# A depthwise convolution split over three engines: one channel tile leaves TensorE, and 24 taps go as ScalarE products to accumulating DMAs

## The reference

```python
h = rms_norm(x, norm_g)
proj = jnp.einsum('bsd,de->bse', h, w_in)
a, bv, bg, z = jnp.split(proj, [A_W, A_W + B_W, A_W + 2 * B_W], axis=-1)
pooled = multiscale_pool(a.reshape(B, S, POOL_GROUPS, POOL_CH))      # trailing means of 2, 4, 8, 16
ya = jnp.einsum('bsgc,gce->bsge', pooled, pool_w).reshape(B, S, A_W) * pool_scale
u = bv * jax.nn.sigmoid(bg)
u = causal_depthwise_conv(u, conv_w, width=31) + conv_b              # one filter per channel
yb = jax.nn.silu(layer_norm(u, cn_g, cn_b))
y = jnp.concatenate([ya, yb], axis=-1) * jax.nn.silu(z)
x = x + jnp.einsum('bse,ed->bsd', y, w_out)
```

## Time and profile before

| | |
|---|---|
| median of 3 runs | 352.47 us (352.41 to 352.56) |
| profiled execution | 352.38 us, its span 350.6 us |
| PE busy | 342.6 us, 98% |
| DVE busy | 268.8 us, 77% |
| ACT busy | 212.7 us, 61% |
| POOL busy | 16.7 us, 5% |
| PE in the chain that ended last | 88% |
| DMA | 54.30 MB, mean 155 GB/s |
| granted clock of PE | full in all 40 slices |

### The profile page before, as it was taken

The page is one execution under the profiler, slowest core; times in us unless marked ns, Lnnn a source line. Parts: engine busy times, 40 slices in busy tenths (PEclk is TensorE's granted clock), DMA queues, the critical chain, the costliest instruction groups (busy, mean ns, idle before and its releaser), DMA issues.

```text
span 350.6 us, 5813 instructions
## 1 busy us (share of the span) xinstructions
PE 342.6 (98%) x2257; PEld 309.8 (88%) x2257; DVE 268.8 (77%) x512; ACT 212.7 (61%) x421; POOL 16.7 (5%) x26
## 2 busy tenths in 40 slices
PE   8999999999999999999999999999999999999995
PEld 8899999999999999998999999988887766688885
DVE  3998798999979999975877699774565686667533
ACT  5759999864239583044474664955359475675440
POOL 0000000000000000000000000004220030400000
PEclk9999999999999999999999999999999999999999
DMA  7896051560505156603625906383641523100003
GB/s 279 372 359 242 1 202 58 221 241 0 215 28 185 62 236 236 244 1 122 257 102 195 387 20 241 120 328 153 239 179 70 207 66 147 53 3 0 3 2 120
DMA packets 8235, 54.30 MB, mean 155 GB/s; under 512 B 912, under 2 KB 1040, under 8 KB 1936
## 3 DMA queue, kind: packets, MB, share of 16 engines
q1 hardware_dynamic: 8064, 53.78, 40.1%
q10 hardware_dynamic: 144, 0.15, 0.2%
HBM read 52.88 MB, written 1.05 MB: 154 GB/s over the span
## 4 chain that ended last, share of the span: by engine, by line
PE 88%; DVE 5%; DMA 2%; ACT 2%; issue 2%; SPq 0%; ACTq 0%; DVEq 0%
PE bank L963 20%; PE bank L965 20%; PE bank L964 20%; PE bank L995 16%; PE bank L1021 6%; DVE w_lo L633 3%; DMA raw<-w 2%; PE bank L1196 2%; PE bank L1206 2%; PE bank L1101 1%; PE bank L1220 1%; DVE scratch L882 1%; DVE scratch L873 1%; PE bank L1175 1%; PE bank L1038 1%
## 5 line engine op out<-in xcount | busy, mean ns | idle before, releaser
L633 DVE TENSOR_TENSOR w_lo<-raw,w_hi 128x1024 fp32r<-128x1024 f32 x76 | 89.2, 1219 | 12.1 <-ACT w_hi L369 12.0
L369 ACT CAST w_hi<-raw 128x1024 fp32r<-128x1024 f32 x76 | 75.3, 1048 | 6.4 <-PE bank L965 4.6
L744 DVE SCALAR_TENSOR_TENSOR scratch<-scratch,params 128x256 f32<-128x256 f32 x142 | 59.2, 476 | 3.5 <-ACT scratch L467 3.3
L963 PE MATMUL bank<-h_hi,w_hi 128*128 128x256 f32 x208 | 60.0, 288 | 0.0
L965 PE MATMUL bank<-h_hi,w_lo 128*128 128x256 f32 x208 | 58.8, 283 | 0.0
L964 PE MATMUL bank<-h_lo,w_hi 128*128 128x256 f32 x208 | 58.8, 283 | 0.0
L995 PE MATMUL bank<-H,raw 128*128 128x256 f32 x256 | 56.8, 379 | 0.9 <-DMA raw<-w 0.9
L995 PEld LDWEIGHTS bank<-H,raw 128*128 128x128 f32 x256 | 48.0, 190 | 7.3 <-DMA raw<-w 1.1
L963 PE MATMUL bank<-ya_hi,w_hi 128*128 128x256 f32 x144 | 42.8, 297 | 0.0
L965 PE MATMUL bank<-ya_hi,w_lo 128*128 128x256 f32 x144 | 40.7, 283 | 0.0
L964 PE MATMUL bank<-ya_lo,w_hi 128*128 128x256 f32 x144 | 40.7, 282 | 0.0
(11 more groups left out here) (116 smaller groups left out, 558.7 us busy)
## 6 DMA issues: line engine op xcount, KB each, us to landing
raw<-w SPq DMA_DIRECT2D x49, 1024.0 KB, 5.4
X<-xT SPq DMA_DIRECT2D x2, 512.0 KB, 5.1
out<-X SPq DMA_DIRECT2D x4, 256.0 KB, 2.7
consts<-const SPq DMA_DIRECT2D x1, 290.0 KB, 13.5
params<-vec ACTq DMA_DIRECT2D x1, 149.0 KB, 4.8
```

The source lines that it names most:

```text
L369: nc.scalar.copy(halves(w_hi, cut_slot(n), half), halves(raw, n % RAW, half)).then_inc(hi_cut, 1)
L633: nc.vector.tensor_tensor(halves(w_lo, cut_slot(n), half), halves(raw, n % RAW, half), halves(w_hi, cut_slot(n), half).bitcast(F32), ALU.s ...
L744: nc.vector.scalar_tensor_tensor(V[:, c, :], U[:, c, k:k + S], column(CW + TAPS * c + k), V[:, c, :], ALU.mult, ALU.add).then_inc(tap, 1)
L963: nc.tensor.matmul(dst, wh, ah, start=start, stop=False, skip_group_check=True)
```

## The change

Tile 7 leaves PE: the diagonals, the hi and lo parts of its taps and of its U, both calls of conv_taps, the read out of PSUM and all semaphores between them are gone. All eight tiles now are done in pairs.

Of pairs 0 and 1 (tiles 0 to 3), the last 12 taps (19 to 30) go another way. In each slot n from 2 on, ACT makes one "side item" for each such pair (12 slots each, from slot 2 and from slot 4): the product of one tap for both tiles, 128 x 512, in two instructions. The items take turns between two sums per pair in side_v. Items 0 and 1 are written to the sums themselves. Items 2 to 11 go to side_ring, and POOL issues a DMA that adds the slot of the ring to the sum (accum_op add), 20 DMAs of 256 KB from SBUF to SBUF. Before item 4 and later ones ACT waits for the DMA of the item two before, and so does POOL. DVE at last adds each of the four sums to V (128 x 512, "folds"), three slots after the last item of the sum or later.

conv_plan is new. It keeps an estimate of the time that DVE and ACT have left in each slot (slot_work) and takes the pair with the most taps left, a product where ACT has time and a single tap per tile where not. It begins at slot 2 instead of 3. It gives, slot by slot (single taps + products + folds): 2: 8, 3: 4+6, 4: 8, 5: 6+6, 6: 8, 7: 8+6, 8: 6, 9: 4+5, 10: 0+1, 11: 2+5, 12: none, 13: 6+3, 14: 4+2, 15: 6+5+1, 16: 8+0+1, 17: 8+0+1, 18: 6+0+1, 19: 10, 20: 12; in all 114 + 39 + 4. Before it was 142 single taps and 34 products, from slot 3 to slot 20.

channel_mean now goes through the tiles in the order 0 to 7. side_ring lies in the bytes of ya_lo, which is not in use in these slots.

```diff
+CONV_PAIRS = tuple((2 * i, 2 * i + 1) for i in range(4))
+SIDE = 2
+SIDE_ITEMS = 12
...
+def side_taps(pair):
+
+    return range(TAPS - SIDE_ITEMS, TAPS) if pair < SIDE else ()
+
+
+def side_items(n):
+
+    return [(pair, n - BG[pair + 1]) for pair in range(SIDE) if 0 <= n - BG[pair + 1] < SIDE_ITEMS]
+
+
+def slot_work(n):
+
+    dve, act = 0, 0.8 * len(side_items(n))
+    if n + 2 not in NATIVE and n < OA[0]:
+        dve, act = dve + 2.3, act + 1.9
+    if n - 1 in BV:
+        dve, act = dve + 0.6, act + 1.0
+    if n - 1 in A:
+        dve += 0.75 * (n - A[0]) + 1.0
+    if n in ZB or n - 1 in ZA:
+        dve, act = dve + 0.8, act + 0.6
+    if n in BG or n in A or n in ZB or n in ZA:
+        act += 0.6
+    if n in (ZB[0], PW):
+        act += 1.3 if n == ZB[0] else 3.2
+    return dve, act
 
 
 def conv_plan():
 
-
-
-
-
-    plan, last, used, count, rest = {}, {}, [], 0, conv_order()
-    for n in range(BV[1], OA[0] + 1):
+    plan, last, used, count, before = {}, {}, [], 0, None
+    left = {pair: [k for k in range(1, TAPS) if k not in side_taps(pair)] for pair in range(4)}
+    folds = list(range(2 * SIDE))
+    dve_time = act_time = 0.0
+    for n in range(BG[1], OA[0] + 1):
         plan[n] = []
-        budget = LONG_SLOT if n in (A[2] + 1, ZB[0] + 1) else SLOT
-        while rest and (budget > 0 or n == OA[0]):
-            g, k = rest[0]
-            tiles = CONV_GROUPS[g]
-            pair = tiles[0] // 2
-            if pair >= n // 2:
+        dve, act = slot_work(n)
+        length = 6.9 if n in NATIVE else 5.75
+        dve_time = min(dve_time, 2.0) + DVE_SHARE * length - dve
+        act_time = min(act_time, 2.0) + ACT_SHARE * length - act
+        while dve_time > 0 or n == OA[0]:
+            here = [pair for pair in left if left[pair] and CONV_PAIRS[pair][0] // 2 < n // 2]
+            if not here:
                 break
-            rest.pop(0)
-            if len(tiles) == 2 and k in PRODUCT_TAPS and pair < (n - 1) // 2 and A[0] - 3 <= n <= LAST_PRODUCT:
+            pair = max(here, key=lambda p: (len(left[p]) - (2 if p == before else 0), -p))
+            before, k, tiles = pair, left[pair].pop(0), CONV_PAIRS[pair]
+            if act_time > 0.8 and pair < (n - 1) // 2 and n <= LAST_PRODUCT:
                 count += 1
                 plan[n].append((tiles, k, len(used), max(last.get(c, 0) for c in tiles), count))
                 used.append(count)
-                budget -= 1.5
+                dve_time, act_time = dve_time - 0.61, act_time - 0.8
                 last.update({c: count for c in tiles})
             else:
                 for c in tiles:
                     count += 1
                     plan[n].append(((c,), k, None, last.get(c, 0), count))
                     last[c] = count
-                    budget -= 1
+                dve_time -= 0.8
+        while folds and n >= BG[folds[0] // 2 + 1] + SIDE_ITEMS + 1 + folds[0] % 2:
+            tiles = CONV_PAIRS[folds[0] // 2]
+            count += 1
+            plan[n].append((tiles, None, folds.pop(0), max(last[c] for c in tiles), count))
+            dve_time -= 0.61
+            last.update({c: count for c in tiles})
...
+        with nc.sbuf_tensor("side_ring", [P, SIDE, 2, 2, S], F32) as side_ring:
+            pass
         ya_lo = sb("ya_lo", [P, KD, S], F32R)
-        taps_hi = sb("taps_hi", [P, TAPS], F32R)
-        taps_lo = sb("taps_lo", [P, TAPS], F32R)
-        u_hi = sb("u_hi", [P, PAD + S], F32R)
-        u_lo = sb("u_lo", [P, PAD + S], F32R)
+        side_v = sb("side_v", [P, SIDE, 2, 2, S])
...
+            for n in range(BG[1], OA[0]):
+                for pair, item in side_items(n):
+                    if item > 1:
+                        pool.wait_ge(side_ready[pair], item + 1)
+                        if item > 3:
+                            pool.wait_ge(side_added[pair][item % 2], 16 * (item // 2 - 1))
+                        pool.dma_start(side_v[:, pair, item % 2, :, :], side_ring[:, pair, item % 2, :, :],
+                                       accum_op=ALU.add).then_inc(side_added[pair][item % 2], 16)
...
-            def build_diagonals(first, last):
-
-                for k in range(first, min(last, TAPS)):
-                    for part, t in zip(diagonals(k), (taps_hi, taps_lo)):
-                        nc.scalar.mul(part, ident, t[:, k:k + 1].bitcast(F32)).then_inc(diag_ready, 1)
+            def side_product(pair, item):
+
+                if item > 3:
+                    act.wait_ge(side_added[pair][item % 2], 16 * (item // 2 - 1))
+                to = (side_ring if item > 1 else side_v)[:, pair, item % 2, :, :]
+                k = side_taps(pair)[item]
+                for i, c in enumerate(CONV_PAIRS[pair]):
+                    last = nc.scalar.mul(to[:, i, :], U[:, c, k:k + S], column(CW + TAPS * c + k))
+                last.then_inc(side_ready[pair], 1)
...
+                for pair, item in side_items(n):
+                    side_product(pair, item)
...
+                    if k is None:
+                        pair, chain = divmod(product, 2)
+                        dve.wait_ge(side_added[pair][chain], 16 * ((SIDE_ITEMS - chain + 1) // 2 - 1))
+                        nc.vector.tensor_tensor(V[:, c:c + 2, :], V[:, c:c + 2, :], side_v[:, pair, chain, :, :],
+                                                ALU.add).then_inc(tap, 1)
+                    elif product is None:
...
-            def conv_taps(a, b):
-
-                pe.wait_ge(ulo_ready, 1)
-                pe.wait_ge(diag_ready, 2 * b)
-                for k in range(a, b):
-                    last = product(bank[5][:, 0:S], diagonals(k), (u_hi[:, k:k + S], u_lo[:, k:k + S]),
-                                   k == 0, k == TAPS - 1)
-                last.then_inc(conv_done, 1)
...
-                if n in (A[2], ZB[0]):
-                    conv_taps(*((0, CONV_CUT) if n == A[2] else (CONV_CUT, TAPS)))
...
-            def channel_mean(tiles):
-                for c in tiles:
-                    if c == CONV_PE:
-                        pe.wait_ge(conv_out, 1)
-                    else:
-                        pe.wait_ge(tap, TILE_DONE[c])
-                    last = nc.tensor.matmul(bank[1][:, 0:S], ones[:, :], V[:, c, :], start=(c == CONV_PE), stop=(c == 6),
+            def channel_mean():
+                for c in range(KD):
+                    pe.wait_ge(tap, TILE_DONE[c])
+                    last = nc.tensor.matmul(bank[1][:, 0:S], ones[:, :], V[:, c, :], start=(c == 0), stop=(c == KD - 1),
                                             skip_group_check=True)
-                if tiles[-1] == 6:
-                    last.then_inc(mean_sum, 1)
+                last.then_inc(mean_sum, 1)
```

More of the change, by code:

```diff
@@ L181, in conv_plan @@
                     last[c] = count
-                    budget -= 1
+                dve_time -= 0.8
[5 more added lines that the diff above has]
+            last.update({c: count for c in tiles})
     return plan, last, used
-SLOT, LONG_SLOT = 10, 14
-PRODUCT_TAPS = range(2, TAPS, 2)
+DVE_SHARE, ACT_SHARE = 0.97, 0.9
 CONV_PLAN, TILE_DONE, PRODUCT_USED = conv_plan()
@@ L226, in hybrid_trunk @@
         dist = C_[:, DIST:DIST + 384]
-        scratch = sb("scratch", [P, 12800])
+        scratch = sb("scratch", [P, 12654])
         at = 0
@@ L246, in hybrid_trunk @@
         FX = part(2 * 15).rearrange("p (c t) -> p c t", c=2)
-        assert at <= 12800
+        assert at <= 12654
         PR = SZ[:, 0:KD, :]
@@ L283, in hybrid_trunk @@
         late = sem("late")
-        taps_cut, uhi_ready, ulo_ready = sem("taps_cut"), sem("uhi_ready"), sem("ulo_ready")
-        diag_ready, conv_done, conv_out = sem("diag_ready"), sem("conv_done"), sem("conv_out")
+        side_ready = [sem(f"side_ready{i}") for i in range(SIDE)]
+        side_added = [[sem(f"side_added{i}{chain}") for chain in range(2)] for i in range(SIDE)]
         sig_ready, u_ready = sem("sig_ready"), sem("u_ready")
@@ L304, in hybrid_trunk @@
         block = ctx.enter_context(nc.Block())
[L306 to L310, removed]
         def column(c, n=1):
@@ L441, in _ @@
                     act.wait_ge(pooled, g + 1)
-                    if g == 0:
-                        act.wait_ge(conv_done, 2)
                     nc.scalar.copy(yb_hi[:, 2 * g:2 * g + 2, :], YP[:, 2 * g:2 * g + 2, :]).then_inc(phi_ready, 1)
                 for tiles, k, product, _, _ in CONV_PLAN.get(n, ()):
-                    if product is None:
+                    if product is None or k is None:
                         continue
@@ L463, in _ @@
                             act.wait_ge(u_ready, n // 2)
-                        if c == CONV_PE:
-                            nc.scalar.copy(u_hi[:, :], U[:, c, :]).then_inc(uhi_ready, 1)
-                        else:
-                            nc.scalar.activation(V[:, c, :], U[:, c, 0:S], ACT.Identity, bias=column(CB + c),
```

(14 more changed lines are left out.)

8 lines of the change are left out of this document (removed).

## The result

The changed kernel takes 343.19 us (median of 4 runs, 343.11 to 343.25), against 352.51 before beside it: a ratio of 0.973 (95% interval 0.9714 to 0.9747), 9.3 us faster. The forecast was 343.0, in a range of 341.0 to 348.5.

What follows compares the result with a forecast made beforehand. PE, busy 258.79 of 259.00 us until the attention stage, was taken as the bound. 352.4 - 11.1 (convolution off PE) + 1.0 (PE waits) + 0.7 (table errors) = 343.0 us, range 341.0 to 348.5.

Steps and rivals of the forecast that it cites:

- PE's 11.08 us: Convolution stage: the two pieces of the convolution on PE, 5.70 + 5.38 us, all on the path, go.
- DVE's table: DVE's work added up per pair of slots, 4 to 15, giving when each w_lo is complete against PE's need.
- the 1.5 that I had allowed: Possible error of the table of DVE's turns: 2% of six turns, 1.5 us.
- PE's waits: PE waiting for w_lo at units 12, 14 and 16: 0.6 + 0.3 + 0.1 = 1.0 us charged.
- due times: When PE, relieved, reaches its units: 59.4 for unit 8, 72.1, 84.7, 97.3, 110.0 for unit 16; last mean matmul 149.9.
- The 0.7 us for errors of the table: Half of a possible 1.5 us error in DVE's turns per pair of slots, added as loss.
- The accumulating DMAs: 20 DMAs of 256 KB issued by POOL: landing taken as 5 us, cost nothing, up to 1; cover about 10 us.
- the limit at 10.7: ACT's ring slots: the 12.66 us turn less product, issue and hand-overs hides a landing of up to 10.7 us.
- The estimate of 2.6 us: Landing of a 256 KB accumulating DMA from about 2.0 us fixed plus bytes over 436 GB/s.
- Rival (a): Elementwise engines become the bound, slips of slots 4 to 13 exceeding the cover: 4.8 us more, 348; chance 0.12.
- Rival (c): POOL's DMA issues hold up DVE: 20 x 1.0 us, less 1 of margin, 362; chance 0.05.
- Rival (d): PE time goes, but a new queue's fixed cost or the mean's wait for folds eats 0 to 11 us; chance 0.05.

Runs made afterwards that it cites:

- Experiment 1: The changed kernel with 93 matmuls, result never used, put back on PE in the places of the old ones: 353.24 us, ratio 1.0023.
- Experiment 8: The changed kernel with 12 side items kept and only the planner's shares moved, to 0.98 for DVE and 0.85 for ACT: 342.60 us, ratio 0.972.
- Experiment 9: The changed kernel with 14 side items per pair in place of 12 and planner's shares 0.96 and 0.8: 341.67 us, ratio 0.9697.
- experiment 7: The changed kernel with one, then two, tiny POOL steps ahead of each accumulating DMA: 348.15 us and 369.35 us.
- experiments 6: The changed kernel with a second, tiny copy DMA behind each of the 20 accumulating ones on POOL's queue: 343.07 us, ratio 0.9733.
- experiment 5: The kernel before with one tiny accumulating DMA (128 x 32 floats, read by nobody) on POOL's queue: 352.41 us, ratio 0.9994.
- either half of this change alone: The changed kernel with PE's 93 matmuls put back, 353.24 us; and the changed kernel with no side items, all taps through DVE, 358.40 us.
- experiment 4: The changed kernel with the 20 accumulating DMAs left out, so the output lacks the taps of items 2 to 11: 343.33 us, ratio 0.9741.
- experiment 2: The changed kernel with no side items: tile 7 leaves PE and DVE takes all taps: 358.40 us, ratio 1.0163.

## Why the prediction was right, point by point

**PE's 11.08 us: right**, by the milestones of the earlier trace rows. Experiment 1 shows that it is the whole gain: put back, it takes 10.05 us, the 9.3 gained and 0.8 more.

**DVE's table: right to about a microsecond, and late on one side.** w_lo complete, by the table and as measured (start of the step behind it): unit 8 57.4 and 57.95, unit 10 72.1 and 73.03, unit 12 85.2 and 86.25, unit 14 98.5 and 99.46, unit 16 110.1 and 110.99. It was 0.5 to 1.05 late each time, within the 1.5 that I had allowed. The last tap: 149.1 and 149.03. The price of a chained product holds: six take 53.38 - 49.05 = 4.3 us, with some of the next tap's wait in it.

**PE's waits: the size right, the places not quite.** I had 0.6 + 0.3 + 0.1 at units 12, 14 and 16; it was 0.16, 0.55, 0.57 and nothing at units 10, 12, 14 and 16, together 1.28. But the charge of 1.0 does not come out of the table. PE needs the first half of w_lo, 1.1 us before it is complete, so by the table's times it would be there at 84.1, 97.4 and 109.0 for due times of 84.7, 97.3 and 110.0: a wait of 0.1. The table's lateness of about 1 us made up the difference, so this agreement is in part luck. The cause of the waits is the one that the prediction named: product-heavy odd slots, in which ACT and DVE turn in 14 to 15 us. Experiment 8 takes three products away from slots 3 to 9 and 0.55 us of the loss goes. Experiment 9 takes six away, with two more side items per pair, and all of it goes but 0.03.

**The 0.7 us for errors of the table: met only in part by them.** Of 1.7 us that I charged, 1.41 were lost before the mean, 0.13 of it at the very start, where I had nothing. Another 0.46 came at a place for which the prediction had nothing, the landing of the last store. So the agreement to 0.2 us is partly two small errors that cancel.

**The accumulating DMAs: right that they cost nothing, wrong on the margin.** I took a landing of 5 us and the limit at 10.7. They land in 3.5 to 5.2 us, or in 7.5 to 10.0 behind a pair of weight loads. The step that failed is the use of the nearest row: 5.4 is the median of 49 loads, and it doesn't show what happens behind two loads issued together, which take 6.1 and 9.4 us in the example above. The estimate of 2.6 us by the Trainium skill ("DMA: Bandwidth & Descriptors", section "Anatomy of one DMA — SWDGE (gpsimd) path") is even below the shortest of 3.5 us. Experiment 1 bears the two groups out. POOL issues at 86.85 and 87.72 there too, but no load is issued between 74 and 90 us, and the landings are 3.7 and 5.2 us instead of 9.4 and 9.9:

```profile
DMA to landing us min/median/max: 3.7/4.4/5.2
```

That there is a limit is shown from two sides: ACT waits for landings of 9.3 to 10.3 us where slots follow each other faster (experiment 9), and with one POOL step more per DMA the time is 348.15 (experiment 7). The 10.7 itself was never tried: it holds for turns of 12.66 us, and the turns are not all that long. The margin was thin where I had called it wide ("cover about 10 us"): 1.3 us at the closest.

**Rival (a)** did not come. **Rival (c)** is refuted for DVE, by experiments 6 and 7: DVE's 114 taps take 47.0 and 46.9 us there, and 46.9 without any DMA. The prediction said that by the Trainium skill's rule this rival would hold. That was too much: the rule is on GpSimd instructions that read SBUF, and no run shows that a DMA issue is one. By the rule of the Trainium skill ("SBUF — State Buffer", section "Who interferes with whom") the one that begins first keeps the other out. In the two rows in which POOL's step began first (254.60 in the earlier trace rows, and 67.58 in experiment 7, by 0.01 us) DVE kept its length, 2.35 for the w_lo pair and 3.26 us for the eight taps, which does not agree. The longest POOL step is no test of it, since DVE's taps were running when it began. **Rival (d)** did not come: no fixed cost of the queue (experiment 5), and DVE has no wait for the sums at the folds.

**Open: the last store.** The longest of the four landings is 2.8 us before, 2.7 with 14 items and with one sum per pair (22 DMAs), 3.2 in the changed kernel and in experiments 1 and 8, and 3.1 without any accumulating DMA. It is not the DMAs; what it is, no run here tells.

## What to carry to other kernels

When one engine is busy nearly all of a stage, what you take off it is the most that you can gain (11.1 us here, of which 9.3 came), and the question is whether the others meet its new due times: add up their work per turn against its turn, and look for the turns that are longer, not at the sum, which fell here. A transfer that adds to a sum can be hidden if the next one to the same sum comes later than its longest landing, and a second sum doubles that time at the price of one addition. Before you take a median for such a landing, look whether it hides two groups, and what was issued just before the slow one. Work taken off an engine that doesn't bound is worth nothing until the one that does is relieved, and the other way round: either half of this change alone is slower than before.

## What the runs showed of the hardware

- An accumulating DMA of 256 KB between two places of SBUF lands in 3.5 to 5.2 us, but in 7.5 to 10.0 when it is issued within 4 us behind two weight loads of 1 MB (changed kernel; experiment 1 has both kinds too, and in experiment 7 one issued 3.5 us behind a pair took only 4.6). POOL issues it in 0.87 us, and the kernel without these DMAs is no faster (experiment 4).
- A POOL step on 128 x 8 floats that takes 1.66 us in the attention stage takes up to 4.44 us beside DVE steps with two SBUF operands, and these do not get longer (experiment 7).
- While PE waited 13.09 us in experiment 2, its granted clock was 0.84 in 148:155 and then 0.50 until 165 us, 0.77 in 165:168 and 1.00 in 168:175, with PE busy from 161.80 on. The eight channel-mean products at the start of this took 5.96 us instead of 3.62.
- A wait of PE that the profile shows as 0.32 us is 0.55 us in the distance between its units, because busy time is pipelined length.
